# Attention as one sequence of 64 query blocks over all heads, with a second set of q and k in halves of the weight buffers

## The reference, cut to what matters

```
def diff_attention(q, k, v, lam, slopes):
    qb = jnp.moveaxis(q.reshape(b, nb, Q_BLOCK, h, 2, d), 1, 0)     # 8 blocks of 128 queries
    def block(args):
        scores = jnp.einsum("bqhrd,bshrd->bhrqs", qi, k).astype(jnp.float32) * scale   # 64 ** -0.5
        dist = jnp.abs((start + jnp.arange(Q_BLOCK))[:, None] - k_pos[None, :])
        scores = scores - slopes[None, :, None, None, None] * dist[None, None, None]
        probs = jax.nn.softmax(scores, axis=-1)
        w = probs[:, :, 0] - lam * probs[:, :, 1]
        return jnp.einsum("bhqs,bshe->bqhe", w.astype(v.dtype), v)
...
    slopes = jnp.exp2(-8.0 * (jnp.arange(ATTN_HEADS) + 1.0) / ATTN_HEADS)
    o = diff_attention(q, k, v, lam, slopes)
    o = rms_norm(o, subln_g) * (1.0 - lam_init)
    y_attn = o.reshape(b, s, D_ATTN) * jax.nn.silu(g)
```

## Time and profile before

| | us |
|---|---|
| median of the runs | 4266.29 |
| the profiled execution's own time | 4264.93 |
| its span | 4263.2 |
| TensorE busy in the span | 3800.3 |
| VectorE busy | 2172.2 |
| ScalarE busy | 1658.7 |
| attention stage, from VectorE's first setting to the last product with the gate | 1762.72 to 2599.59 |

### The profile page before, as it was taken

How to read it: one execution, slowest core, us unless ns; L and a number is a source line. 1 busy time by engine, 2 the same in 40 slices (tenths; PEclk the granted TensorE clock), 3 DMA queues, 4 the chain that set the end, 5 groups by cost and what they waited for, 6 DMA issues and landing times.

```text
span 4263.2 us, 48828 instructions
## 1 busy us (share of the span) xinstructions
PE 3800.3 (89%) x20470; PEld 3142.5 (74%) x20470; DVE 2172.2 (51%) x2817; ACT 1658.7 (39%) x2227; POOL 528.8 (12%) x437
## 2 busy tenths in 40 slices
PE   6989999999988999788888876989888898879998
PEld 5768978878766777666666655988777777768988
DVE  3444243343464667355445443357777777743222
ACT  4323121212234556465556653133444544431122
POOL 0000010100000536000000000012222222210002
PEclk9989999999998999899999997999999999999999
DMA  2002011111111010100000003121111111143111
GB/s 88 30 26 80 31 65 50 50 40 50 50 41 60 22 48 21 50 25 25 25 25 25 25 15 153 40 80 40 40 40 40 35 40 45 37 157 132 40 31 65
DMA packets 196399, 211.31 MB, mean 50 GB/s; under 512 B 7944, under 2 KB 171733, under 8 KB 196181
## 3 DMA queue, kind: packets, MB, share of 16 engines
q1 hardware_dynamic: 190420, 187.22, 13.8%
q10 hardware_dynamic: 5760, 20.97, 1.3%
HBM read 174.62 MB, written 33.55 MB: 49 GB/s over the span
## 4 chain that ended last, share of the span: by engine, by line
PE 66%; DVE 16%; ACT 11%; issue 5%; DMA 1%; POOL 0%; SPq 0%; ACTq 0%; DVEq 0%; POOLq 0%
PE pd L211 57%; PE pq L211 7%; ACT t L2343 2%; DVE t L2395 2%; ACT t L311 2%; DVE t L320 2%; DVE t L2723 2%; PE pd L354 1%; PE pq L354 1%; DVE t L3126 1%; DVE t L2715 1%; DVE t L1788 1%; DVE t L2413 0%; DVE t L3111 0%; ACT L2379 0%
## 5 line engine op out<-in xcount | busy, mean ns | idle before, releaser
L211 PE MATMUL pd<-t 128*128 128x512 f32 (+2 forms) x15920 | 3118.8, 356 | 118.2 <-DVE t L602 33.4
L211 PEld LDWEIGHTS pd<-t 128*128 128x128 f32 x15920 | 2576.5, 193 | 600.1 <-issue 145.1
L211 PE MATMUL pq<-t 128*128 128x128 f32 (+5 forms) x3222 | 571.4, 340 | 133.6 <-DVE t L2395 37.8
L211 PEld LDWEIGHTS pq<-t 128*128 128x128 f32 (+2 forms) x3222 | 398.8, 185 | 263.1 <-DVE t L2395 58.3
L311 ACT ACTIVATE t<-t 128x2048 fp32r<-128x2048 f32 (+2 forms) x134 | 241.6, 1804 | 752.8 <-PE pd L211 667.9
L320 DVE TENSOR_TENSOR t<-t 128x2048 fp32r<-128x2048 f32 (+2 forms) x134 | 295.9, 2209 | 366.8 <-ACT t L311 366.7
L354 PE MATMUL pd<-t 128*128 128x128 f32 x800 | 131.2, 314 | 118.2 <-DVE t L2413 32.4
L1388 DVE TENSOR_TENSOR t<-pd,t 128x512 f32<-128x512 f32 x256 | 171.8, 690 | 122.8 <-PE pd L211 122.8
L354 PEld LDWEIGHTS pd<-t 128*128 128x128 f32 x800 | 109.7, 164 | 145.1 <-ACT t L2224 35.0
L2343 ACT ACTIVATE t<-t 128x1024 f32<-128x1024 f32 x128 | 146.2, 1143 | 94.1 <-DVE t L2400 94.1
L2723 DVE SCALAR_TENSOR_TENSOR t<-t 128x1024 f32<-128x1024 f32 x120 | 180.0, 1500 | 0.3
(11 more groups left out here) (286 smaller groups left out, 2809.7 us busy)
## 6 DMA issues: line engine op xcount, KB each, us to landing
t<-in_w_in_dram SPq DMA_DIRECT2D x97, 512.0 KB, 5.0
t<-in_w_mlp_dram SPq DMA_DIRECT2D x32, 1024.0 KB, 5.3
t<-in_w_out_dram SPq DMA_DIRECT2D x20, 1024.0 KB, 5.2
t<-in_w_in_dram SPq DMA_DIRECT2D x16, 1024.0 KB, 5.3
t<-ym_scratch ACTq DMA_DIRECT2D x24, 512.0 KB, 7.9
t<-in_x_dram SPq DMA_DIRECT2D x16, 512.0 KB, 7.7
x_scratch<-t SPq DMA_DIRECT2D x16, 512.0 KB, 2.8
ym_scratch<-t SPq DMA_DIRECT2D x16, 512.0 KB, 2.6
```

The source lines that it names most:

```text
L211: ins = e.matmul(out, l, r, start=(first and j == 0), stop=(last and j == n - 1), skip_group_check=True)
```

## The change

- q and k have two sets: odd heads keep tiles of their own, even heads use columns 1024 to 2047 of `WH`, `WL` and so also of the memory of `WR`. A weight unit of attention is therefore 128 columns (1024 columns of the buffers), one kind of one head: 32 units in place of 16. The unit of g of head 0 gets its turns in `ssm_out(1)`.
- `att_stage` and its weaving go. One loop on each engine runs over 64 blocks n. In block n TensorE makes scores(n+2), one projection product of the next head (`KIND[tt]`: k, k, q, q, v, v, g, g), a transposition of values at tt 6 and 7, the `oms` that is owed (`owed`: at tt 2 that of the last head's second half, at tt 5 that of the first half), `AV` of blocks n-4 to n-1 at tt 0 and 4, and last the transposes of block n.
- The bias is made once. q is scaled by 2^(h-2) when it is copied, and the reduction scales by 2^-(h+1).
- The ring `tmp` has four buffers in place of two.

```
 def act_ssm_out(e, g):
+        if g == 1:
+            act_unit(e)
...
 def dve_ssm_out(e, g):
+        if g == 1:
+            dve_unit(e)
...
 def sp_ssm_out(e, g):
+        if g == 1:
+            sp_unit(e)
...
+    QS = [[w[:, 1024:2048] for w in WH], [sbt(ph, [128, S], F32R) for _ in range(2)]]
+    KS = [[w[:, 1024:2048] for w in WL[0:2]], [sbt(ph, [128, S], F32R) for _ in range(2)]]
+    KL = [[WL[2][:, 1024:2048], sbt(ph, [128, S], F32R)], [sbt(ph, [128, S], F32R) for _ in range(2)]]
-    tmp = ring(ph, 2, [128, 512])
+    tmp = ring(ph, 4, [128, 512])
...
+    def act_att_out(e, h, kind, th):                      # ScalarE, after the product of this kind
+        if kind in "qk" and h >= 2:
+            e.wait_ge(*at["scores", h - 2, 7, 1])
+        if kind == "k":                                   # four copies of 64 x 512
+            e.copy(K[0][LO, sl], b[LO, :]) ... e.copy(K[1][HI, sl], b[HI, :]) ...
+            e.copy(K[0][HI, sl], b[LO, :]) ... e.copy(K[1][LO, sl], b[HI, :]) ... free=("ak", h, th)
+        elif kind == "q":                                 # two
+            e.mul(Q[0][LO, sl], b[LO, :], 2.0 ** (h - 2)) ... e.mul(Q[1][HI, sl], ...) ... free=("aq", h, th)
+        elif kind == "v": e.copy(vT[:, :], b[:, :]) ... free=("av", h, th)
+        else: e.activation(gT[:, sl], b[:, :], ACT.Silu) ... free=("ag", h, th)
+    def dve_att_out(e, h, kind, th):                      # VectorE, k and q only: two 64 x 512
+        if kind == "k": e.wait_ge(*at["kcc", h, th]) ... e.tensor_tensor(L[1][HI, sl], ...) ... free=("ak", h, th)
+        elif kind == "q": e.wait_ge(*at["qh", h, th]) ... e.scalar_tensor_tensor(...) ... free=("aq", h, th)
...
+    def pe_stage_att(e):
+        for th in range(2):
+            pe_att_vt(e, 0, th)
+            if th == 0:
+                pe_att_unit(e, 0, "k")
+            pe_att_fm(e, 0, "k", th)
+        pe_att_unit(e, 0, "q")
+        for th in range(2):
+            pe_att_fm(e, 0, "q", th)
+        pe_att_scores(e, 0)
+        pe_att_scores(e, 1)
+        for n in range(BLOCKS):
+            h, tt = divmod(n, NT)
+            if n + 2 < BLOCKS:
+                pe_att_scores(e, n + 2)
+            if h < 7:
+                if tt % 2 == 0:
+                    pe_att_unit(e, h + 1, KIND[tt])
+                pe_att_fm(e, h + 1, KIND[tt], tt % 2)
+                if tt >= 6:
+                    pe_att_vt(e, h + 1, tt - 6)
+            pe_att_ms(e, *owed(n))
+            if tt % 4 == 0 and n:
+                pe_att_values(e, n - 4)
+            for q2 in range(2):
+                b = e.take(PD, "wT", n, q2)
+                e.wait_ge(*at["diff", n])
+                ... transposed(...) ...
+        pe_att_values(e, 60)
+        pe_att_ms(e, 7, 1)
+    def act_stage_att(e):
+        ...
+        for n in range(BLOCKS):
+            if n + 1 < BLOCKS: scaled(n + 1)
+            if n + 2 < BLOCKS: scores(n + 2)
+            e.wait_ge(*at["wT", n, 0])
+            e.copy(WT[:, 0:4, tile(tt % 4)], ...)
+            if tt % 4 == 0 and n:
+                act_att_values(e, n - 4)
+            act_att_ms(e, *owed(n))
+            if h < 7:
+                act_att_out(e, h + 1, KIND[tt], tt % 2)
+                if tt >= 6:
+                    act_att_vt(e, h + 1, tt - 6)
+                if tt % 2 == 0:
+                    if (h, tt) == (6, 6):
+                        e.wait_ge(*at["scores", 6, 7, 1])
+                    act_unit(e)
+    def dve_stage_att(e):
+        ...
+        for n in range(BLOCKS):
+            mixed(n)
+            if n + 1 < BLOCKS: scaled(n + 1)
+            if n + 2 < BLOCKS: scores(n + 2)
+            e.wait_ge(*at["wT", n, 1])
+            e.tensor_copy(WT[:, 4:8, tile(tt % 4)], ...)
+            if h < 7:
+                dve_att_out(e, h + 1, KIND[tt], tt % 2)
+                if tt % 2 == 0:
+                    dve_unit(e)
+            if tt in (3, 6):
+                dve_att_ms(e, *owed(n - 1))
```

More of the change, by code:

```diff
@@ L2192, in pe_att_first, with pe_att_fm, pe_att_vt @@
+    def pe_att_fm(e, h, kind, th):
+        fm(e, open_unit[-1], 0, th, 2, "a" + kind, h, th)
+        if th == 1:
+            pe_done(open_unit[-1])
+    def pe_att_vt(e, h, th):
+        b = e.take(PD, "avT", h, th)
+        e.wait_ge(*at["avc", h, th])
+        transposed(e, b, [tmp.of("avc", h, th)[:, tile(j)] for j in range(4)]).then_inc(
+            *at.inc("pe", "avT", h, th, free=("avc", h, th)))
     def pe_att_first(e):
-        u = pe_unit(e, W2in, [(4640, 128), (5664, 128)])
-        for kind, m0 in (("av", 0), ("ag", 128)):
+        for kind in "vg":
+            pe_att_unit(e, 0, kind)
@@ L2196, in pe_att_first @@
             for th in range(2):
[L2197 to L2216, removed]
@@ L2218, in act_att_vg @@
-    def act_att_vg(e, h):
-        gT, vt_ = AB[h % 2]
-        act_unit(e)
-        for th in range(2):
-            vT = e.take(tmp, "avc", h, th)
[L2223 to L2233, removed]
+                pe_att_fm(e, 0, kind, th)
@@ L2283, in pe_att @@
[L2283 to L2301, removed]
-        scores(0)
[L2304 to L2339, removed]
[L2340 to L2352 removed]
+            e.activation(gT[:, sl], b[:, :], ACT.Silu).then_inc(*at.inc("act", "agt", h, th, free=("ag", h, th)))
@@ new lines, in program, with pe_att_scores @@
+    BLOCKS = 64
+    def pe_att_scores(e, n):
+        h, tt = divmod(n, NT)
+        Q, K, L = QS[h % 2], KS[h % 2], KL[h % 2]
+        for ks in range(2):
+            e.wait_ge(*at["kcc", h, ks])
+            e.wait_ge(*at["kl", h, ks])
+        for r in range(2):
+            e.wait_ge(*at[f"KL{r}"])
+        e.wait_ge(*at["qh", h, tt // 4])
+        e.wait_ge(*at["ql", h, tt // 4])
+        for sh in range(2):
+            for r in range(2):
+                if n:
+                    e.wait_ge(*at["smax", n - 1, r])
+                mms(e, PQt[r][:, half(sh)], [(Q[r][:, tile(tt)], K[r][:, half(sh)]),
+                                             (Q[r][:, tile(tt)], L[r][:, half(sh)])]).then_inc(
+                    *at.inc("pe", "scores", h, tt, r))
@@ new lines, in owed, with pe_att_ms, pe_att_values @@
+    def owed(n):
+        h, tt = divmod(n, NT)
+        return {2: (h - 1, 1), 5: (h, 0)}.get(tt, (-1, 0))
+    def pe_att_ms(e, h, th):
+        if h >= 0:
+            b = e.take(PD, "oms", h, th)
+            e.wait_ge(*at["osq", h, th])
+            mms(e, b[:, :], [(ones[:, :], tmp.of("osq", h, th)[:, :])]).then_inc(*at.inc("pe", "oms", h, th))
+    def pe_att_values(e, n):
+        h, th = n // 8, n // 4 % 2
+        b = e.take(PD, "AV", h, th)
+        for m in range(n, n + 4):
+            for q2 in range(2):
+                e.wait_ge(*at["wTc", m, q2])
+        e.wait_ge(*at["avt", h, 0])
+        e.wait_ge(*at["avt", h, 1])
+        mms(e, b[:, :], [(AB[h % 2][1][:, j, :], WT[:, j, :]) for j in range(8)]).then_inc(*at.inc("pe", "AV", h, th))
@@ new lines, in act_att_ms, with act_att_values @@
+    def act_att_ms(e, h, th):
+        if h >= 0:
+            q = tmp.of("osq", h, th)
+            e.wait_ge(*at["oms", h, th])
+            e.wait_ge(*at["epsc"])
+            e.activation(q[:, :], PD.of("oms", h, th)[:, :], ACT.Ln, scale=1.0 / 128, bias=epsc[:, 0:1]).then_inc(
+                *at.inc("act", "oln", h, th, free=("oms", h, th)))
+            e.wait_ge(*at["oln", h, th])
+            e.activation(q[:, :], q[:, :], ACT.Exp, scale=-0.5).then_inc(*at.inc("act", "ors", h, th))
+    def act_att_values(e, n):
+        h, th = n // 8, n // 4 % 2
+        b = PD.of("AV", h, th)
+        o = e.take(tmp, "o", h, th)
+        q = e.take(tmp, "osq", h, th)
+        e.wait_ge(*at["AV", h, th])
+        e.activation(q[:, :], b[:, :], ACT.Square).then_inc(*at.inc("act", "osq", h, th))
+        e.copy(o[:, :], b[:, :]).then_inc(*at.inc("act", "o", h, th, free=("AV", h, th)))
@@ new lines, in act_stage_att, with scores, scaled @@
+    def act_stage_att(e):
+        def scores(n):
+            s, x = SR.of("s", n), sm.of("x", n)
+            for r in range(2):
+                e.wait_ge(*at["smn", n])
+                e.activation(s[:, r, :], s[:, r, :], ACT.Exp, bias=x[:, 2 + r:3 + r],
+                             accum_out=x[:, 4 + r:5 + r]).then_inc(*at.inc("act", "sexp", n))
+        def scaled(n):
+            s, x = SR.of("s", n), sm.of("x", n)
+            e.wait_ge(*at["srec", n])
+            e.mul(s[:, 0, :], s[:, 0, :], x[:, 6:7]).then_inc(*at.inc("act", "p0", n))
+        act_unit(e)
+        for th in range(2):
+            act_att_out(e, 0, "v", th)
+        act_unit(e)
+        act_att_vt(e, 0, 0)
+        for th in range(2):
+            act_att_out(e, 0, "g", th)
+        act_att_setup(e)
+        act_att_out(e, 0, "k", 0)
+        act_att_vt(e, 0, 1)
+        act_att_out(e, 0, "k", 1)
+        act_unit(e)
+        for th in range(2):
+            act_att_out(e, 0, "q", th)
+        scores(0)
@@ L2386, in dve_att @@
-    def dve_att(e, h):
-        gT, vt_ = AB[h % 2]
-        def scores(tt):
```

(55 more changed lines are left out.)

214 lines of the change are left out of this document (88 added, 126 removed).

## The result

The changed kernel takes **4295.2 us** (median of four runs, 4292.97 to 4296.57), the one before 4265.4 beside it: a ratio of 1.0069 with a 95% interval of 1.0051 to 1.0086. It is slower by 30 us; 4297 was forecast. The profiled execution's span is 4291.2 (4263.2 before), the mean granted clock 0.946 (0.951).

The account below looks back on a forecast made before the run. TensorE was taken as the fullest engine, busy 89% of the span. Seven heads +44.4, start -5.7 and last head -7.2 give +31.5 on 4264.93; with 1.4 for the median, 4297 us, range 4240 to 4322.

Parts of the forecast that it names:

- The order gives the drain's time back in front of the projections: Within a head: the boundary drain goes, but its time returns as waits before projections; 103.2 us a head at full clock.
- The four stalls: TensorE's waits for product readers in a head: second k 3.6, second q 8.2, first g 4.8, next head's first k 3.5.
- The fifth item: Scores waiting for reductions, at the second v and second g products of a head: 1.8 us together.
- Half clock behind each: TensorE at half clock after each of four stalls in a head: 2.0 us each, 8.0 together, 1.1 hidden in the longest.
- The rival in which the clock holds: Stalls stay in the heads but TensorE runs at full clock behind them: 4245 us, chance 0.13.
- A head of 110.0: One middle head: 81.3 us of work, 21.9 of stalls, plus half clock; the seven heads together +44.4.
- Start and last head: The ends of the attention stage: -5.7 us up to the first transposes, -7.2 in the last head.
- The edits at nothing: Turns of g's unit, half-width units, waits for scores, q's scaling and four tmp buffers cost nothing; 8.6 us covers g's turns.
- What the prediction cites: Skill rules: pauses between PSUM groups cost half clock (used); table switches cost 2.66 us with a 1.38 drain (not used).
- A ring that does not stall: Rival: each product's readers finish before its PSUM buffer is needed again; a head is 81.3 plus some 5; 4148 us, chance 0.07.
- Half of it: Rival: second q stall 4 in place of 8, one stall keeps the clock; head 104, within 9 us of before; chance 0.11.
- slow throughout: Rival: 2.8 us for each stall, and growing waits at second v and g products: 4320 us or more, chance 0.14.

Follow-up runs that it names:

- e2: The changed kernel with oms taking its PSUM buffer ahead of the block's projection product on TensorE: 4238.70 us, 0.9933 of the kernel before.
- e4: The changed kernel with ScalarE's copies of the projection product ahead of the exponentials, and Ln and Exp at the block's end: 4152.51 us, 0.9732 of the kernel before.
- e1: The changed kernel with Ln and Exp moved from ahead of the copies to the end of ScalarE's block: 4229.75 us, 0.9913 of the kernel before.
- e6: The changed kernel with oms ahead of the projection on TensorE and Ln and Exp at the end of ScalarE's block: 4254.32 us, 0.9965 of the kernel before.
- e7: e4 with VectorE's subtractions moved ahead of its copy of the transposed weights: 4144.04 us, 0.9713 of the kernel before.

## Why the prediction was right, point by point

- **The order gives the drain's time back in front of the projections.** Right, and shown by e2: the order of takes alone, with every other engine's program untouched, moves 57 us.
- **The four stalls.** Forecast 3.6, 7.1 (8.2 less what half clock hides), 4.8 and 3.5; the profile has 3.09, 6.79, 4.28 and 3.43, for the engines named. For the first and third, part of the difference is where the count starts: the forecast counts from T+2.6 (its own terms, 0.8 + 1.9, give 2.7), the profile from the end of the scores' record, T+2.9 (1916.80 for a T of 1913.91). The readers themselves were done at T+6.0 for 6.2 forecast and T+7.2 for 7.4. The fifth item, 1.8 of waits at the second v and g products, was too large: the profile has 0.40 for the scores and 0.31 for Silu. All waits are 18.3 for 20.8 forecast (21.9 less 1.1), and matmuls with their pipeline ends fill 1.8 more than the 81.3 counted. These two misses nearly cancel in the head; some 1.0 of it is the same time, the ends ahead of the four waits, which the forecast counted as waiting, and the rest is luck.
- **Half clock behind each.** Forecast 2.0 for each, 8.0 a head. The runs behind the four waits took 1.7, 3.0, 1.7 and 1.7 longer than 5.6 (12.5 for the one with AV), 8.1 in sum. The rival in which the clock holds is out. (Its terms in the prediction, from 708, 45.5 and 58 to 61, add up to -25 to -22 and not to -22 to -20, so 4241 to 4244 in place of 4245; the range held it either way.)
- **A head of 110.0.** 109.5. The first interval came as forecast, 100.6 (1813.29 to 1913.91). The seven together gave +40.6 and not +44.4: the five heads are 109.2 to 109.5, 3.3 less than forecast together, and the last interval is 104.0 in place of 104.5. This is the term that was mis-sized, by 3.8.
- **Start and last head.** -4.7 and -8.2 for -5.7 and -7.2; each is off by 1.0, on opposite sides. That they cancel is luck.
- **The total.** The profiled executions differ by 28.0 for 31.5 forecast. The median of the changed kernel lies 2.2 above its profiled execution where the forecast added 1.4, so 4295.2 came nearer to the forecast than the parts did. The sum itself is 4297.8, which was written as 4297.
- **The edits at nothing.** TensorE's products of the scan that stand before the turn of g's unit already come 0.8 later in this execution (1715.07 for 1714.28), and the transposes behind that turn are 0.8 later too (1753.02 for 1752.25). So the turn adds nothing that shows, as the cover of 8.6 promised.
- **What the prediction cites.** The trace agrees in kind with the Trainium skill ("TensorE: Matmul & The Clock Gate", section "A second HAM failure mode: psum-queue depth-cycling"): a granted clock of 0.91 in the head with four stalls, 1.00 in that of e4. But a price at each such pause, as the prediction drew from it, held in the changed kernel and not in e1, e2 and e6 (last section). The Trainium skill ("ScalarE: Activation LUTs", section "What ACT_TABLE_LOAD costs") puts a drain of 1.38 beside each load; here the copy ends at 1939.25, the load starts at 1939.27 and Ln at 1940.57, with no room for a drain, and q's stall of 6.79 has no 2.8 more in it.
- **The other rivals.** A ring that does not stall (4148) is what the kernel becomes once the copies are ahead and Ln and Exp last, 4144 to 4152 (e4, e7), but not what the change is. "Half of it" and "slow throughout" would have needed a head of 104 or 113.

Not tried: whether the kernel before, with one set of q and k, would gain as much from the same orders; a ring of another size or one of its own for the projection products; and a filler for the stalls, which would need a PSUM buffer that is not free in them.

## What to carry to other kernels

A ring of buffers that many kinds of results share ties the producer to the slowest reader of the result n takes back, so count, for each take, which result that is and where its reader stands in its own engine's list; a scheme without any drain can lose to one with a drain by this alone. Then read a shared buffer early: putting its copies (and VectorE's subtractions) ahead of work whose result is needed later, and Ln and Exp behind them, turned 4295 into 4144 us here without removing an instruction. Two such moves can undo part of each other (e6), so recount the takes after each.

## What the runs showed of the hardware that was not expected

A wait of the same length did not always bring half clock: behind 3.10 the 24 matmuls took 7.34 in e1 and 5.75 in e6's head above; behind 2.87 they took 5.74 in e1, behind 2.59 7.36 in e6. It differs even at one place of one run, from head to head. In e2, the next head's first k product with AV:

```profile
1897.26 12.60 PE L211 MATMUL pd<-t 128*128 128x512 f32 x40 [3.43 <-ACT t L2252]
...
1996.64 14.20 PE L211 MATMUL pd<-t 128*128 128x512 f32 x40 [3.42 <-ACT t L2252]
```

In the changed kernel itself every one of the four waits was followed by half clock in all the heads from block 8 to block 47. So 2.0 a stall was right there as a mean, and nothing here says which single stall pays it: what decides is open.
